# Adaptive-norm modulation computed in column tiles and spread over three places of a two-block transformer kernel

## The reference

```python
s_lat = jax.nn.silu(c)[:, None, :]
s_ctx = jax.nn.silu(c_ctx)
for l in range(DEPTH):                      # DEPTH = 2, D = 1024
    mod = jnp.split(s_lat @ w_ada[l] + b_ada[l], 6, axis=-1)     # w_ada[l]: 1024 x 6144
    modc = jnp.split(s_ctx @ w_ada[l] + b_ada[l], 6, axis=-1)
    h = _modulate(_rmsnorm(x, norm1_g[l]), mod[0], mod[1])
    hc = _modulate(_rmsnorm(xc, norm1_g[l]), modc[0], modc[1])
    p = h @ w_in[l]
    ...
    x = x + mod[2] * _mixer_merge(p, ml_x, *mix_args)
    h = _modulate(_rmsnorm(x, norm2_g[l]), mod[3], mod[4])
    x = x + mod[5] * _peer(h, *peer_args)
```

## Time and profile before

| | us |
|---|---|
| median of 3 runs | 4991.02 (4985.24 to 4991.22) |
| the profiled execution's own time | 4996.75 |
| its span, first to last instruction | 4995.0 |
| `fresh_modulation`, first load issued to the next stage's first instruction | 17.98 to 123.45 |
| `branch_inputs` of layer 0 | 151.0 to 263.2 |
| the 12 steps with `ada` in layer 0's expert stage | 1485 to 1704 |

### The profile page before, as it was taken

One profiled execution on the slowest core, in us unless ns is written; L12 is line 12 of the kernel. 1 busy time (PEld: TensorE's weight loads), 2 busy tenths in 40 slices (PEclk: granted clock), 3 DMA queues, 4 the chain that ended last, 5 costly groups with the idle time before them and its releaser, 6 DMA issues. The chain is left out here.

```text
span 4995.0 us, 60626 instructions
## 1 busy us (share of the span) xinstructions
PE 4427.7 (89%) x24318; PEld 3695.3 (74%) x24318; DVE 2616.1 (52%) x5014; ACT 1666.8 (33%) x2046; POOL 924.7 (19%) x222
## 2 busy tenths in 40 slices
PE   7889989999999999999779889899978758966688
PEld 1766568888875688888667789888867758865587
DVE  0644458787830244444564699526664445522465
ACT  0333123333331222222343444444443124431343
POOL 0322024332332100000242565530000200000000
PEclk9899999999999999999889999999988879976799
DMA  7232213455465565555343456678852025440254
GB/s 251 77 106 72 76 69 123 131 177 177 174 237 193 173 207 189 198 190 196 96 133 129 153 169 228 243 234 283 282 197 80 5 78 157 145 139 22 89 157 139
DMA packets 453172, 770.71 MB, mean 154 GB/s; under 512 B 19982, under 2 KB 324142, under 8 KB 432634
## 3 DMA queue, kind: packets, MB, share of 16 engines
q1 hardware_dynamic: 452268, 764.68, 46.3%
q10 hardware_dynamic: 624, 2.15, 0.2%
HBM read 663.37 MB, written 103.38 MB: 154 GB/s over the span
## 5 line engine op out<-in xcount | busy, mean ns | idle before, releaser
L1401 POOL TENSOR_TENSOR pr_wlo<-pr_w,pr_whi 128x2048 fp32r<-128x2048 f32 x142 | 668.3, 4707 | 1077.6 <-ACT pr_whi L1514 1077.6
L113 PE MATMUL bank<-hThi_l,pr_whi 128*128 128x512 f32 (+1 forms) x2304 | 791.3, 343 | 45.3 <-POOL pr_wlo L1401 35.3
L113 PE MATMUL bank<-hTlo_l,pr_whi 128*128 128x512 f32 (+1 forms) x2304 | 779.3, 338 | 0.0
L113 PE MATMUL bank<-hThi_l,pr_wlo 128*128 128x512 f32 (+1 forms) x2304 | 779.1, 338 | 0.0
L113 PE MATMUL bank<-pr_whi,pr_ahi 128*128 128x512 f32 x1536 | 598.9, 390 | 7.3 <-DVE pr_alo L1675 7.1
L1514 ACT ACTIVATE pr_whi<-pr_w 128x2048 fp32r<-128x2048 f32 x270 | 515.3, 1908 | 252.1 <-DMA pr_w<-peer_v_in 236.5
L113 PE MATMUL bank<-pr_whi,pr_alo 128*128 128x512 f32 x1536 | 597.7, 389 | 0.0
L113 PE MATMUL bank<-pr_wlo,pr_ahi 128*128 128x512 f32 x1536 | 597.6, 389 | 0.0
L1652 DVE TENSOR_SCALAR pr_hot<-iota,pr_choice 128x128 f32<-128x128 f32 x768 | 465.1, 606 | 107.6 <-PE bank L1449 93.9
L113 PEld LDWEIGHTS bank<-hThi_l,pr_whi 128*128 128x128 f32 x2304 | 442.0, 192 | 103.8 <-POOL pr_wlo L1401 39.6
L113 PEld LDWEIGHTS bank<-hThi_l,pr_wlo 128*128 128x128 f32 x2304 | 441.7, 192 | 45.7
(11 more groups left out here) (482 smaller groups left out, 8376.9 us busy)
## 6 DMA issues: line engine op xcount, KB each, us to landing
pr_w<-peer_u_in SPq DMA_DIRECT2D x128, 1024.0 KB, 5.8
pr_w<-peer_v_in SPq DMA_DIRECT2D x128, 1024.0 KB, 5.0
dense_weights<-pr_buf SPq DMA_DIRECT2D x12, 4096.0 KB, 17.3
gu_w<-ffn_w_up_in SPq DMA_DIRECT2D x88, 512.0 KB, 5.3
mx_w<-w_in_in SPq DMA_DIRECT2D x32, 1024.0 KB, 5.0
expert_scores<-pr_s SPq DMA_DIRECT2D x64, 512.0 KB, 6.9
pr_gs<-expert_scores SPq DMA_DIRECT2D x64, 512.0 KB, 5.8
pr_g<-dense_weights SPq DMA_DIRECT2D x64, 512.0 KB, 7.1
```

Source lines behind the costliest of these rows:

```text
L113: ins = pe.matmul(psum, a, b, start=first and i == 0, stop=last and i == len(terms) - 1)
L1401: pool.tensor_tensor(w_lo[:, n % ring, :, :], wt[:, n % ring, :, :], w_hi[:, s, :, :].bitcast(F32), ALU.subtract).then_inc(lo_ready, 1)
```

## The change

**One chunk as column tiles.** `column_tiles` takes the place of the 8 matmuls per chunk. For each of the 8 row blocks `k` it issues four matmuls of 128 weight columns each; the result of number `j` goes to partitions 32j and 32j+1 of the bank instead of all to partitions 0 and 1. The bias is now four matmuls of one row by 128 columns everywhere (in the first stage VectorE added it). So a chunk is 36 matmuls of 128 columns, where it was 8 (first stage) or 9 (expert stage) of 512. Emptying the bank takes four copies of 2 x 128 instead of one operation of 2 x 512, and storing it four transfers instead of one.

**Where the chunks are computed.** Of layer 0, chunks 0 to 3 stay in `fresh_modulation`, which now has four weight buffers and issues all four loads at once. Chunks 4 to 9 move into `branch_inputs` of layer 0 (`ModulationBeside`): chunk i is fetched by SyncE right behind weight part i+2 and computed by TensorE behind part i+2, in banks 6 and 7, which `project` does not use; ScalarE copies it, SyncE stores it. Chunks 10 and 11 of a layer are computed in its own expert stage, ahead of the next layer's. So in layer 0 the expert stage still computes 12 chunks (two of its own, ten of layer 1), in steps 52 to 63; in layer 1 it computes two, in steps 50 and 51. Over the whole kernel there are still 24.

```diff
+                if side and n - ahead < side.chunks:
+                    side.fetch(sp, n - ahead)
+                    if n - ahead >= 2:
+                        side.store(sp, n - ahead - 2)
+            if side:
+                for i in range(side.chunks - 2, side.chunks):
+                    side.store(sp, i)
+                side.finish(sp)
...
+                if side and i + 1 == ends[n] and 0 <= n - ahead < side.chunks:
+                    side.rows(pe, n - ahead)
...
+                    if side and 0 <= n - ahead < side.chunks:
+                        side.copy(eng, n - ahead)
...
+def column_tiles(pe, bank, s_cols, w, b, ones):
+
+    for k in range(KD):
+        for j in range(4):
+            pe.matmul(bank[32 * j:32 * j + 2, 0:P], s_cols[:, k, :], w[:, k, j * P:(j + 1) * P], start=k == 0, stop=False)
+    for j in range(4):
+        last = pe.matmul(bank[32 * j:32 * j + 2, 0:P], ones[0:1, 0:2], b[:, j * P:(j + 1) * P], start=False, stop=True)
+    return last
...
-    n_chunks = 6 * D // 512
-    with nc.sbuf_tensor(f"ada_w{l}", [P, 2, KD, 512], F32) as wt, nc.sbuf_tensor(f"ada_b{l}", [2, 6 * D], F32) as ball, \
-            nc.sbuf_tensor(f"ada_row{l}", [2, 2, 512], F32) as row:
...
+    n_chunks = 4
+    with nc.sbuf_tensor(f"ada_w{l}", [P, 4, KD, 512], F32) as wt, nc.sbuf_tensor(f"ada_b{l}", [1, 4 * 512], F32) as ball, \
+            nc.sbuf_tensor(f"ada_row{l}", [P, 4, P], F32) as row:
...
                 for n in range(n_chunks):
-                    if n >= 2:
-                        sp.wait_ge(row_ready, n - 1)
-                    sp.dma_start(wt[:, n % 2, :, :], w[:, n * 512:(n + 1) * 512].rearrange("(k p) n -> p k n", p=P))\
-                      .then_inc(loaded[n % 2], 16)
+                    sp.dma_start(wt[:, n, :, :], w[:, n * 512:(n + 1) * 512].rearrange("(k p) n -> p k n", p=P)).then_inc(loaded[n], 16)
                     if n == 0:
-                        sp.dma_start(ball[:, :], K.dram["b_ada"][l:l + 1, :].broadcast_to([2, 6 * D])).then_inc(bias_in, 16)
+                        sp.dma_start(ball[:, :], K.dram["b_ada"][l:l + 1, 0:4 * 512]).then_inc(bias_in, 16)
...
+                pe.wait_ge(bias_in, 16)
                 for n in range(n_chunks):
-                    pe.wait_ge(loaded[n % 2], 16 * (n // 2 + 1))
-                    if n >= 2:
-                        pe.wait_ge(row_sum, n - 1)
-                    for k in range(KD):
-                        last = pe.matmul(K.ps[n % 2][0:2, :], s_cols[:, k, :], wt[:, n % 2, k, :], start=k == 0, stop=k == KD - 1)
-                    last.then_inc(row_ready, 1)
+                    pe.wait_ge(loaded[n], 16)
+                    column_tiles(pe, K.ps[n], s_cols, wt[:, n, :, :], ball[:, n * 512:(n + 1) * 512], K.ones).then_inc(row_ready, 1)
...
+                    for j in range(4):
+                        rows = slice(32 * j, 32 * j + 2)
+                        last = dve.tensor_copy(row[rows, n, :], K.ps[n][rows, 0:P])
+                    last.then_inc(row_sum, 1)
...
+                    for j in range(4):
+                        act.dma_start(chunk_of(K, l, n, j), row[32 * j:32 * j + 2, n, :]).then_inc(row_stored, 16)
+                    if n % 2:
+                        c = n // 2
+                        act.wait_ge(row_stored, 64 * (n + 1))
+                        for s in range(2):
+                            act.dma_start(mod[c][:, s, :], K.ada[l, s:s + 1, c * D:(c + 1) * D].broadcast_to([P, D])).then_inc(mod_in, 16)
...
+class ModulationBeside:
...
+    first, chunks = 4, 6
...
+    def fetch(self, sp, i):
+        if i >= 2:
+            sp.wait_ge(self.ready, i - 1)
+        cols = slice((self.first + i) * 512, (self.first + i + 1) * 512)
+        sp.dma_start(self.w[:, i % 2, :, :], self.K.dram["w_ada"][self.l][:, cols].rearrange("(k p) n -> p k n", p=P)).then_inc(self.loaded[i % 2], 16)
+        sp.dma_start(self.b[:, i % 2, :], self.K.dram["b_ada"][self.l:self.l + 1, cols]).then_inc(self.loaded[i % 2], 16)
+
+    def store(self, sp, i):
+        sp.wait_ge(self.copied, i + 1)
+        for j in range(4):
+            sp.dma_start(chunk_of(self.K, self.l, self.first + i, j), self.row[32 * j:32 * j + 2, i % 2, :]).then_inc(self.stored[i % 2], 16)
+
+    def finish(self, sp):
+        for s in range(2):
+            sp.wait_ge(self.stored[s], 64 * (self.chunks // 2))
+
+    def rows(self, pe, i):
+        pe.wait_ge(self.loaded[i % 2], 32 * (i // 2 + 1))
+        if i >= 2:
+            pe.wait_ge(self.copied, i - 1)
+        column_tiles(pe, self.K.ps[6 + i % 2], self.K.s_cols, self.w[:, i % 2, :, :], self.b[:, i % 2, :], self.K.ones).then_inc(self.ready, 1)
+
+    def copy(self, act, i):
+        act.wait_ge(self.ready, i + 1)
+        if i >= 2:
+            act.wait_ge(self.stored[i % 2], 64 * (i // 2))
+        for j in range(4):
+            at = slice(32 * j, 32 * j + 2)
+            last = act.activation(self.row[at, i % 2, :], self.K.ps[6 + i % 2][at, 0:P], ACT.Copy)
+        last.then_inc(self.copied, 1)
...
+    own = 2
+    n_ada = n_chunks if nxt else own
...
+    def layer_chunk(c):
+        return (l, n_chunks - own + c) if c < own else (l + 1, c - own)
...
-                        sp.dma_start(K.ada[l + 1, :, c * 512:(c + 1) * 512], ada_row[:, c % 2, :]).then_inc(row_stored[c % 2], 16)
-                if nxt:
-                    for s in range(2):
-                        sp.wait_ge(row_stored[s], 16 * (n_ada // 2))
+                        for j in range(4):
+                            sp.dma_start(chunk_of(K, *layer_chunk(c), j), ada_row[32 * j:32 * j + 2, c % 2, :]).then_inc(row_stored[c % 2], 16)
+                for s in range(2):
+                    sp.wait_ge(row_stored[s], 64 * (n_ada // 2))
...
-                    for k in range(KD):
-                        pe.matmul(K.ps[4 + c % 2][0:2, :], K.s_cols[:, k, :], ada_w[:, c % 2, k, :], start=k == 0, stop=False)
-                    pe.matmul(K.ps[4 + c % 2][0:2, :], K.ones[0:1, 0:2], ada_b[:, c % 2, :], start=False, stop=True).then_inc(row_ready, 1)
+                    column_tiles(pe, K.ps[4 + c % 2], K.s_cols, ada_w[:, c % 2, :, :], ada_b[:, c % 2, :], K.ones).then_inc(row_ready, 1)
...
+                    for j in range(4):
+                        at = slice(32 * j, 32 * j + 2)
+                        last = act.activation(ada_row[at, c % 2, :], K.ps[4 + c % 2][at, 0:P], ACT.Copy)
+                    last.then_inc(row_copied, 1)
...
+        side = ModulationBeside(K, l, upper) if l == 0 else None
```

65 lines of the change are left out of this document (33 added, 32 removed).

## The result

The changed kernel takes **4881.6 us** (median of four runs, 4871.8 to 4882.8) where the kernel before takes 4991.1 (four runs, 4985.2 to 4995.5): a ratio of 0.9777, 95% interval 0.976 to 0.9794, 2.2% faster. Repeated twice beside other runs, the ratio was 0.9761 (0.9745 to 0.9777) and 0.976 (0.9747 to 0.9772). One execution of the second repeat took 5175.3 us at a granted clock of 0.807, where the others had 0.93, and is left out of every comparison. The profiled execution of it has a span of 4870.0 us, against 4995.0.

The account below looks back on a forecast made before the run. TensorE, busy 89% of the span, was taken as the main bound. First stage -67, branch_inputs +19.4, layer 0's expert stage -45 and layer 1's +14 summed to -78.6 us: 4912 us from the 4991.02 median, range 4875 to 5008.

Parts of the forecast that it names:

- rival (a): TensorE's chunk matmuls: all four partition groups run abreast, T = 2.4, whole kernel 4872 us; chance 0.15.
- T: Price of one chunk after the change, in us: taken as 4.3, bounded between 2.4 and 8.25.
- The lower end: Chunk on TensorE: four tiles run abreast, 18 x 0.109 = 1.96 us of passes, giving T = 2.4.
- The middle case: Chunk on TensorE: only one matmul's last pass and the next one's first overlap, 36 x 0.109 = 3.9, T = 4.3.
- if starts keep program order: TensorE premise: passes start in program order, so only neighbouring matmuls' last and first passes overlap, giving T = 4.3.
- First stage: Stage ends at 56.8 instead of 123.45 us: -67; -69 at T = 2.4, -51 at T = 8.25.
- 6T - 6.4: `branch_inputs` of layer 0: six chunks less TensorE's spare 6.4 us; +19.4 forecast, +8 and +43 at the ends.
- rival (c): Feed stalls: weight parts late in `branch_inputs` (+12) and again in layer 1 (+10), whole kernel 4934 us; chance 0.08.
- 12 x (T - 8.12) + 1: Layer 0's expert stage: 12 chunks at T instead of 8.12, plus 1 for a slow first chunk; -45 forecast.
- the forecast's +14 for 4.3: Layer 1's expert stage: two chunks added behind the 4 MB store wait, +14 us at T = 4.3.
- The slope: Whole kernel: the summed time rises by 24 us per microsecond of T.
- Rival (b): TensorE's chunk matmuls: no overlap, the four tiles go one after another, T = 8.25, whole kernel 5007 us; chance 0.26.

Follow-up runs that it names:

- one_tile: Changed kernel with each chunk's four 128-column pieces side by side in partitions 0 and 1, bias first as one 512-column matmul: 5009.0 us.
- tile_by_tile: Changed kernel with the matmul loops exchanged, all eight of one partition group in a row before the next group's: 4959.8 us.
- early_loads: Changed kernel with the two preceding stages merged into its first, chunk loads issued first, and layer 1's own two chunks six steps later: 4864.3 us.

## Why the prediction was right, and where it was not

The direction and the range (4875 to 5008) held, but the range only just and by luck: its lower bound cut through rival (a), priced at 4872 and given 0.15, and (a) is what came true. The first comparison gave 4881.6, 30 us below the point forecast of 4912; the repeats gave 4875.5 and 4872.3, and the last of these lies outside the range.

**The step that failed is the choice of T, 4.3 for a measured 2.41.** The lower end, 18 x 0.109 + 0.4 = 2.4, is what TensorE does. The middle case rested on two premises. The first holds: the second pass of a float32 matmul does not run beside the first on the same tile (no two starts closer than 0.108 us in one_tile). The second, "if starts keep program order", fails: in the changed kernel four groups start together every 0.109 us, which leaves no place for both passes of one matmul among the four, and in tile_by_tile a group's first passes start ahead of three passes that stand before them in the program. A busy group's passes don't hold back the next group's until four are waiting, and a float32 matmul has only two. The other support, the closest starts in the earlier trace rows at 0.06 us, was no floor for other forms: starts in different groups are less than 0.01 us apart.

On the two pages of the Trainium skill: that different tiles work in parallel ("TensorEngine Tiling (Array Packing)", section Tiling Modes) agrees with T = 2.41. That matmuls start and end in program order ("TensorE: Matmul & The Clock Gate", section The mechanism) does not agree with the starts of tile_by_tile, and the measurement decides. The cost of the changes of mode is inside the 0.4 us beside the passes, no more than before.

**The rest of the sum held.** The forecast's sum and rival (a)'s are 40 us apart, not 41. At T = 2.4 the prediction had -69, +8, -68 and +10; measured were -67.6, +7.4, -65.5 and +11.3, and in the repeats -67.3, +7.1, -69.8, +10.5 and -67.5, +7.5, -68.9, +10.5.

- First stage: -67 at T = 4.3 and -69 at 2.4 were close together because the loads bound it. The last chunk was there at 43.4 instead of 41.7, and at the low clock a chunk's passes took 2.8 to 3.6 us instead of 1.93. Only the last chunk's delay counts, 0.9 us.
- `branch_inputs`: 6T - 6.4 gives 8.1, 21.3, 31.7 and 43.1 for T = 2.41, 4.61, 6.35 and 8.25; measured 7.4, 20.1, 31.1 and 42.7. TensorE became the bound and waited for nothing after its first matmul, so the feed did not stall and rival (c) has nothing for it here.
- Layer 0: 12 x (T - 8.12) + 1 held within about 3 us in every run: -67.5 was due at T = 2.41 and -65.5 to -70.2 came, +2.6 was due in one_tile and +5.7 came. The 1 us for a slow first chunk was not needed, since the first chunk lost as much before (8.60 for 7.03, now 3.42 for 1.93).
- Layer 1: the idle time on the load came as said (12.95 us where about 14 was forecast), though TensorE's idle time there grew by only 5.0 us, and the rest of the price is the two chunks themselves: +10.5 to +11.3 at 2.41, +18.2 at 4.30, +14.3 at 4.61, +16.0 at 6.35 and +23.9 at 8.25. Less 2T that leaves 3 to 10 us, so the forecast's +14 for 4.3, 5.4 beside the chunks, lies inside the scatter, which is too wide to confirm it.
- The slope, 24 us per microsecond of T: from T = 2.41 to 8.25 the span rises by 5007.2 - 4869.8 = 137.4, which is 23.5 for each, from two single profiles.
- Rival (b) was the right price (5007 predicted, 5009.0 for one_tile) for a mechanism that does not happen when the groups differ.

## What to carry to other kernels

When a matmul's stationary operand has few columns, put neighbouring matmuls into different groups of 32 partitions and change the group with every matmul: here that made 1.66 us of 6.88, and the same matmuls with eight or four in a row per group kept 81% and 56% of the old time. Moving work out of a stage that the loads could bound pays only if it is cheap where it goes; measure the two halves of such a change apart, since -83 and +7 made -120, and give the simpler half its buffers before judging it, since four instead of two made its 83 into 94. Behind a stop of SyncE for a large store, a small load queued behind large ones is as late as they are; ask of each added load what SyncE has just been held up by.

## What was not expected of the hardware

- Two passes of each float32 matmul in the same group did not hold back the other groups: 64 passes into four groups took 1.66 us from first start to last, four starting within 0.02 us every 0.109 us, and every 0.055 us with half the columns.
- Each change of group in the order gave back 0.43 us, once (3 changes) and again (7), about four passes of 0.109, and in the trace the next group's first pass starts ahead of three passes that stand before it in the program.
- With two buffers of 2 MB and almost no work per chunk, loads came at 6.66 us each and the queues moved 340 GB/s; with four, 384 GB/s without a stop, of which the read-back of the rows took its part, so the loads came at 5.90.
- The rows were read back 4.2 to 4.3 us behind the issue of the last small store while large loads ran (chunk 1 in the changed kernel, the last chunk in early_loads), and 1.1 us behind it with the queues quiet.
- The issue of a 2 KB row held SyncE for 5.64 us and, in layer 0, 7.35 us, behind loads of 2 MB.
